# Head of the norm-fed stages widened to four outputs, norm and gate rows moved to PSUM, attention's maximum and scaling regrouped

## The chip, the cores and the metric

The kernel runs on one core of one Trainium2 chip. The metric is device time in microseconds (us) of one execution; lower is better. Input and output are float32, and matmuls take either float32 operands or pairs of float16 parts.

## The reference, cut to what matters

Two transformer blocks run one after the other on a sequence of 512 tokens of width 1024.

```
x   : (1, 512, 1024)
h   = rms_norm(x, g_norm1) * (1 + scale1) + shift1
q, k, v, index rows, pool rows, gates = split(h @ w_in)
y   = sparse attention: 8 heads of 64, 128 keys picked for each query, one k/v head
x   = x + gate1 * ((g_attn * (y @ w_up_attn) + g_pool * (pool @ w_up_pool)) @ w_out)
h2  = rms_norm(x, g_norm2) * (1 + scale2) + shift2
x   = x + gate2 * peer_ffn(h2)          # 16384 experts, 16 of them per head, 8 heads
# second block, two layers
layer 0: windowed attention, 16 heads, 4 k/v heads, distance term slope_h * |i - j|,
         a sink logit per head inside the softmax, window 128 to either side
layer 1: latent attention, 16 heads of 64 + 32 rotary columns, all 512 keys
each layer: h = h + (o * silu(z)) @ w_out
            h = h + (p @ ple_w) * sigmoid(rms_norm(h, ple_norm) @ ple_w_gate)
out = rms_norm(h, final_norm)
```

## The kernel before, in words

Features lie on the 128 partitions: `xT` and `hT` hold 8 blocks of 128 features by 512 tokens. SyncE loads weight tiles of 128x1024 float32 into a ring of 4; POOL cuts each (`cut_tile`, lines 588 to 591) into a high and a low float16 part in a second ring of 4, `parts`; TensorE (PE) multiplies three of the four products of parts (`three`, the matmuls of line 639) and adds them up in PSUM. The order of the tiles is fixed by a plan of stages (`make_plan`), written once and walked by all engines in the same order.

A stage of kind "features" has for each output block `m` its own tile, and runs `m` by `m`, each over 8 input blocks `k`: 24 matmuls of 128x512 for one output. Its sums go to PSUM banks 0 to 3 in turn (`bank`). POOL cuts the tile of output `n` only when PE has begun output `n - 3` (semaphore `begun`), since that is when the slot of output `n - 4` is free. A stage of kind "tokens" runs the other way: for each `k` it adds to four token blocks at once.

A norm works like this. ACT squares the rows of `xT` (line 1014), PE sums them over the partitions with a matrix of ones (`norm_part`, line 689) into bank 7, in `features` stages behind the outputs (`behind`, one part after each output from the third on). ACT takes the root (line 1023), DVE the reciprocal (line 1253). Then for each `k` DVE makes the normed row (`normed`, line 1256) in `whole`, a pair of SBUF rows, ACT writes its high part to `hT` (line 1008 or 1037), and DVE writes the low part (`low`, line 1264 or 1266) and signals `h_ready`. The next stage waits for `h_ready` of block `k` while it runs its first output. The root row and `whole` lie in SBUF (`spare`). The first norm also has, for each `k`, one block of the modulation product on DVE (`modulate`, line 1347, a custom multiply-and-add over 1024 columns with an accumulator).

An attention (`attention` on each engine) walks units of one head and one block of 128 queries, with `w` keys: 128 to 512 in the sparse one (32 units), 256 or 384 in the window one (64 units), 512 in the latent one (64 units). PE's order is fixed: scores of unit `u` (line 738), transposes of the probabilities of `u - 1` (line 747), values of `u - 2` (line 758). DVE adds the mask (1305) or the distance term (1310) in one instruction and takes the negated maximum in a second (1313); in the window one a third, tiny one takes the minimum with the negated sink (1316). ACT takes the exponentials with their sum (1056), in the window one after one of the sink (1053), and copies the transposed probabilities out of PSUM (1008). DVE then adds the sink's term (1325), takes the reciprocal of the sum (1326) and scales the unit's 128x64 output (1328).

After the two later attentions `gate_turned` multiplies each transposed output block by its gate (1668) into `whole` and cuts it into parts (1286, 1287); the stages `a_out` and `b_out` read these. The stages `ple_g0` and `ple_g1` read a norm and give the sigmoid gates (ACT, 1192), which DVE multiplies by the embedding (1684) and adds to `xT` (1686).

## Time and profile before

| what | value |
|---|---|
| median of 3 runs | 2720.87 us (2720.87 to 2723.99) |
| the profiled execution, its own time | 2717.65 us |
| its span, first to last instruction | 2715.8 us |
| mean granted clock of TensorE | 0.968 of full speed |
| share of the chain that ended last | PE 76%, DVE 14%, POOL 3%, issue 3%, ACT 2%, DMA 2% |
| PE busy | 2513.6 us, 93% |
| DVE busy | 1573.1 us, 58% |
| ACT busy | 597.0 us, 22% |
| POOL busy | 1602.8 us, 59% |

Stages in the span, in us from its start: the first norm and the stage `q` 22 to 69, sparse attention 249 to 309, `out` to 420, `peer_q` 429 to 479, the experts to 1893, `a_q` 1902 to 1951, window attention 2016 to 2145, `a_out` 2156 to 2205, `ple_w0` and `ple_g0` 2206 to 2273, the latent projections 2284 to 2409, latent attention 2412 to 2571, `b_out` 2580 to 2630, `ple_w1` and `ple_g1` to 2698, the final norm and the output to the end. Busy time counts only instructions that occupy an engine; an engine can be busy and still wait for another within a stage, so each stage is read by what its slowest chain consists of.

### The profile page before, as it was taken

The numbers are of one execution on the slowest core, as the hardware profiler recorded it, in microseconds if no ns is written. First come the engines' busy times: TensorE is split into PE (matmuls) and PEld (weight loads), VectorE is DVE, ScalarE is ACT, GpSimd is POOL, SyncE is SP. The second block draws the span as 40 slices with busy tenths as digits, with TensorE's granted clock in tenths as the row PEclk, the third lists the DMA queues.
The fourth block names the chain that finished last, engine by engine and source line by source line (L and its number), as shares of the span: only waits on it lengthen the run. The fifth ranks groups of instructions, "written<-read, shape, count | busy, mean of one in ns | idle before, by whom it ended". The sixth has DMA issues, their size and how long they took to land.

```text
span 2715.8 us, 38740 instructions
## 1 busy us (share of the span) xinstructions
PE 2513.6 (93%) x12856; PEld 1259.4 (46%) x12856; DVE 1573.1 (58%) x2831; ACT 597.0 (22%) x1250; POOL 1602.8 (59%) x1048
## 2 busy tenths in 40 slices
PE   4998958999999999999999999999998898999997
PEld 1544523444455555544444444444455533557743
DVE  7896736999877777418822222241228745565534
ACT  2112201211122222211111111111125322245422
POOL 5774137899966666789966666660650166830063
PEclk8998978999999999999999999999999999999998
DMA  6222054355548578688755555550220022310021
GB/s 242 86 86 101 1 209 171 113 153 159 152 128 252 165 222 254 191 277 274 259 203 201 201 201 203 204 203 1 95 78 1 17 73 74 102 54 1 9 78 39
DMA packets 189253, 375.46 MB, mean 138 GB/s; under 512 B 13536, under 2 KB 79200, under 8 KB 189152
## 3 DMA queue, kind: packets, MB, share of 16 engines
q1 hardware_dynamic: 119696, 332.64, 36.3%
q10 hardware_dynamic: 69456, 41.49, 5.2%
q8 instruction: 61, 1.00, 0.2%
q14 instruction: 40, 0.33, 0.0%
HBM read 302.77 MB, written 71.30 MB: 138 GB/s over the span
## 4 chain that ended last, share of the span: by engine, by line
PE 76%; DVE 14%; POOL 3%; issue 3%; ACT 2%; DMA 2%; SPq 0%; DVEq 0%; POOLq 0%; ACTq 0%
PE ps L639 63%; PE ps L738 3%; PE ps L758 3%; PE ps L747 2%; PE ps L870 2%; DVE arena L1347 1%; PE ps L689 1%; DVE spare L1256 1%; POOL ring L589 1%; DVE arena L1465 1%; DVE arena L1464 1%; DVE arena L1286 1%; DVE arena L1313 1%; ACT arena L1056 1%; DVE spare L1253 1%
## 5 line engine op out<-in xcount | busy, mean ns | idle before, releaser
L639 PE MATMUL ps<-hT,parts 128*128 128x512 f16 x4800 | 1068.6, 382 | 38.8 <-DVE hT L1264 22.4
L588 POOL TENSOR_SCALAR parts<-ring 128x1024 f16<-128x1024 f32 x261 | 298.1, 1142 | 873.5 <-PE ps L639 791.6
L639 PEld LDWEIGHTS ps<-hT,parts 128*128 128x128 f16 x4800 | 465.7, 98 | 613.6 <-issue 31.8
L639 PE MATMUL ps<-arena 128*128 128x512 f16 x3072 | 668.2, 381 | 6.9 <-DVE arena L1634 6.9
L591 POOL TENSOR_TENSOR parts<-ring,parts 128x1024 f16<-128x1024 f32 x261 | 573.9, 2199 | 21.8
L639 PEld LDWEIGHTS ps<-arena 128*128 128x128 f16 x3072 | 301.5, 98 | 374.5 <-issue 16.1
L1629 DVE TENSOR_TENSOR arena<-arena 128x512 f32<-128x512 f32 x128 | 144.1, 1126 | 433.4 <-DMA arena<-gate_mem 430.5
L589 POOL TENSOR_SCALAR ring<-ring 128x1024 f32<-128x1024 f32 x261 | 310.5, 1190 | 0.0
L609 POOL TENSOR_TENSOR arena<-ring,arena 128x1024 f16<-128x1024 f32 x128 | 283.1, 2212 | 10.7
L639 PE MATMUL ps<-arena,parts 128*128 128x512 f16 x876 | 207.3, 396 | 46.7 <-POOL parts L591 32.5
L607 POOL TENSOR_SCALAR arena<-ring 128x1024 f16<-128x1024 f32 x128 | 148.0, 1157 | 171.0 <-PE ps L639 171.0
L1120 ACT ACTIVATE spare<-ps 128x512 f32<-128x512 f32 x128 | 76.4, 597 | 575.1 <-PE ps L639 307.6
L1159 ACT ACTIVATE arena<-arena 128x512 f16<-128x512 f32 x128 | 80.5, 630 | 520.8 <-DVE arena L1629 520.7
L1008 ACT ACTIVATE arena<-ps 128x512 f32<-128x512 f32 (+6 forms) x250 | 125.7, 517 | 184.5 <-PE ps L639 182.6
L639 PEld LDWEIGHTS ps<-arena,parts 128*128 128x128 f16 x876 | 87.3, 101 | 169.6 <-issue 59.4
L1605 DVE TENSOR_TENSOR xT<-xT,ps 128x1024 f16<-128x1024 f16 x64 | 78.2, 1221 | 84.8 <-PE ps L870 84.8
L1634 DVE TENSOR_TENSOR arena<-arena 128x512 f16<-128x512 f32 x128 | 122.0, 954 | 5.8 <-ACT arena L1159 5.8
L747 PE MATMUL ps<-ident,arena 128*128 128x128 f32 x496 | 88.2, 289 | 24.2 <-ACT arena L1056 24.0
L747 PEld LDWEIGHTS ps<-ident,arena 128*128 128x128 f32 x496 | 56.8, 142 | 108.4 <-ACT arena L1056 87.2
L639 PE MATMUL ps<-parts,hT 128*128 128x512 f16 (+3 forms) x480 | 73.7, 316 | 33.0 <-DVE hT L1266 23.3
L1310 DVE SCALAR_TENSOR_TENSOR arena<-arena,ps 128x256 f32<-128x256 f32 (+1 forms) x64 | 31.1, 487 | 112.2 <-PE ps L738 110.3
L1014 ACT ACTIVATE hT<-xT 128x512 f32<-128x512 f32 x40 | 24.5, 626 | 297.3 <-DVE xT L1504 217.9
(175 smaller groups left out, 2491.9 us busy)
## 6 DMA issues: line engine op xcount, KB each, us to landing
ring<-w SPq DMA_DIRECT2D x133, 512.0 KB, 3.2
ring<-u SPq DMA_DIRECT2D x128, 512.0 KB, 3.9
ring<-v SPq DMA_DIRECT2D x128, 512.0 KB, 3.3
act_mem<-spare SPq DMA_DIRECT2D x128, 256.0 KB, 3.9
gate_mem<-arena ACTq DMA_DIRECT2D x4, 8192.0 KB, 42.7
arena<-act_mem SPq DMA_DIRECT2D x128, 256.0 KB, 3.6
arena<-gate_mem SPq DMA_DIRECT2D x128, 256.0 KB, 3.8
arena<-ada_w SPq DMA_DIRECT2D x48, 512.0 KB, 6.0
```

The lines of the kernel that those rows point to most:

```text
L588: G.tensor_scalar(dst[:, 0, :], src, WS, 1.0, ALU.mult, ALU.mult).then_inc(scaled, 1)
L589: G.tensor_scalar(src, src, WS, 1.0, ALU.mult, ALU.mult).then_inc(scaled, 1)
L591: G.tensor_tensor(dst[:, 1, :], src, dst[:, 0, :], ALU.subtract).then_inc(parts_ready, 1)
L607: G.tensor_scalar(dst[:, 0, :], src, 1.0, 1.0, ALU.mult, ALU.mult).then_inc(v_high, 1)
L609: G.tensor_tensor(dst[:, 1, :], src, dst[:, 0, :], ALU.subtract).then_inc(parts_ready, 1)
L639: ins = [T.matmul(out_, a, b, start=start and j == 0, stop=stop and j == 2) for j, (a, b) in enumerate(((lhs[0], rhs[0]), (lhs[0], rhs[1]) ...
L738: T.matmul(ps[:, 4 + u % 2, 0:rhs.shape[-1]], lhsT, rhs, start=True, stop=True).then_inc(logits, 1)
L747: mm = T.transpose(ps[:, 6 + u % 2, c * P:(c + 1) * P], probs_b[:, u % 2, c * P:(c + 1) * P], ident[:, :])
L758: mm = T.matmul(ps[:, u % 2, 0:64], pt[:, u % 2, c * P:(c + 1) * P], value_rows(un, un["c0"] + c), start=(c == 0), stop=(c == un["nc"] - 1))
L1008: return A.activation(dst, src, ACT.Copy, scale=scale)
L1629: V.tensor_tensor(prod[:, at % 2, :], pair[:, at % 4, 0, :], pair[:, at % 4, 1, :], ALU.mult).then_inc(product, 1)
L1634: V.tensor_tensor(w_parts[:, at, 1, :], prod[:, at % 2, :], w_parts[:, at, 0, :], ALU.subtract).then_inc(weighted, 1)
```

## The change

Three parts. First, a function `features_wide` runs the first four outputs of a stage together: for `k` 0 to 4 it adds to outputs 0 to 3 at once, then it finishes output 0, 1, 2, 3 over `k` 5 to 7, and the last four run as before. `peer_q`, `a_q`, `a_out`, `ple_g0`, `b_out` and `ple_g1` use it. The parts of the norm's sum come in pairs after outputs 5, 6 and 7. Second, the reciprocal root, the normed rows, the gate rows and the gated row lie in PSUM banks 7, 5 and 6, and 4; `gate_turned` multiplies in place in PSUM. Third, in the sparse and the window attention one `tensor_tensor_reduce` adds the mask or distance and takes the minimum of the negated sum (window: starting from the negated sink, with queries scaled by a per-head factor `steep` at `a_q`'s copy); the sinks' exponentials and, in all three attentions, the reciprocals and the output scaling are done once for eight units, whose values lie side by side in one PSUM bank.

```diff
+        whole_root = ps[:, 7, :]
+        def normed_row(k):
+            return ps[:, 5 + k % 2, :]
+        def gate_row(m):
+            return ps[:, 5 + m % 2, :]
+        gated_row = ps[:, 4, :]
...
+            def features_wide(name, rhs, need, after=None):
+                st = stages[name]
+                early, side = 5, 4
+                def unit(m, k):
+                    return three(bank(st.s0 + m), piece(st.t0 + m, k * P, P), rhs(k), k == 0, k == KC - 1)
+                for k in range(early):
+                    need(k)
+                    for m in range(side):
+                        if k == 0:
+                            need_bank(st.s0 + m)
+                            need_tile(st.t0 + m)
+                        first, last = unit(m, k)
+                        if k == m == 0:
+                            first.then_inc(begun, 1)
+                for m in range(st.outs):
+                    if m >= side:
+                        need_bank(st.s0 + m)
+                        need_tile(st.t0 + m)
+                    for k in range(early if m < side else 0, KC):
+                        if m == 0:
+                            need(k)
+                        first, last = unit(m, k)
+                        if m > 0 and k == (early if m < side else 0):
+                            first.then_inc(begun, 1)
+                    last.then_inc(summed, 1)
+                    if after is not None:
+                        after(m)
...
+            def late_pairs(n):
+                def after(m):
+                    for k in range(2 * (m - 5), 2 * (m - 5) + 2):
+                        if m >= 5:
+                            norm_part(n, k)
+                return after
...
-                    if u0 + u >= 2:
-                        pe.wait_ge(o_ready, u0 + u - 1)
+                    if u % EIGHT == 0 and u0 + u >= 2 * EIGHT:
+                        pe.wait_ge(o_ready, (u0 + u) // EIGHT - 1)
+                    at = place(un) * 64
                     for c in range(un["nc"]):
-                        mm = T.matmul(ps[:, u % 2, 0:64], pt[:, u % 2, c * P:(c + 1) * P],
+                        mm = T.matmul(ps[:, u // EIGHT % 2, at:at + 64], pt[:, u % 2, c * P:(c + 1) * P],
...
-            features("peer_q", hr, h_need(1))
+            features_wide("peer_q", hr, h_need(1))
...
-            features("a_q", hr, h_need(2))
+            features_wide("a_q", hr, h_need(2))
...
-            features("a_out", in_parts(az), lambda k: pe.wait_ge(turned_read, t_a + k + 1), behind(3, 2))
+            features_wide("a_out", in_parts(az), lambda k: pe.wait_ge(turned_read, t_a + k + 1), late_pairs(3))
...
-            features("ple_g0", hr, h_need(3), behind(4, 2))
+            features_wide("ple_g0", hr, h_need(3), late_pairs(4))
...
-                    if un["kind"] == "window":
-                        own.do(A.activation(sm[:, 8 + u % 4:9 + u % 4],
-                                            rows2[:, ROWS2["sink"][0] + un["h"]:ROWS2["sink"][0] + un["h"] + 1],
-                                            ACT.Exp, bias=sm[:, u % 4:u % 4 + 1]))
+                    own.do(A.activation(probs_b[:, u % 2, 0:w], src, ACT.Exp, bias=peak(un, u),
+                                        scale=1.0 if un["kind"] == "latent" else -1.0, accum_out=total(un, u)), probs)
+                    if un["kind"] == "window" and u % EIGHT == EIGHT - 1:
+                        act.wait_ge(sink_shifted, u // EIGHT + 1)
+                        own.do(A.activation(eight_sinks(u), eight_sinks(u), ACT.Exp), sink_exps)
...
-            take("a_q", lambda s, b: copy(aq[:, s, :], b, scale=0.125 / WS))
+            act.wait_ge(rows2_loaded, 16)
+            steep = ROWS2["steep"][0]
+            take("a_q", lambda s, b: copy(aq[:, s, :], b, scale=rows2[:, steep + s:steep + s + 1]))
...
-                own.link(V.reciprocal(root, root))
+                own.link(V.reciprocal(whole_root, root))
                 def normed(k, dst, signal):
-                    own.do(V.scalar_tensor_tensor(out=dst, in0=xT[:, k, :], scalar=g_of(k), in1=root,
+                    own.do(V.scalar_tensor_tensor(out=dst, in0=xT[:, k, :], scalar=g_of(k), in1=whole_root,
...
-                    src = whole[:, k % 2, :]
+                    src = normed_row(k)
...
                     if un["kind"] == "sparse":
-                        own.link(V.tensor_tensor(soft_b[:, u % 2, 0:w], src, mask[:, un["i"], 0:w], ALU.add))
-                        src = soft_b[:, u % 2, 0:w]
+                        own.do(V.tensor_tensor_reduce(out=soft_b[:, u % 2, 0:w], in0=src, in1=mask[:, un["i"], 0:w],
+                                                      scale=-1.0, scalar=HIGHEST, op0=ALU.add, op1=ALU.min,
+                                                      accum_out=peak(un, u)), max_ready)
                     elif un["kind"] == "window":
...
+                        if u % EIGHT == EIGHT - 1:
+                            own.settle()
+                            a_ = ROWS2["sink"][0] + un["h"] - (EIGHT - 1)
+                            own.do(V.tensor_tensor(eight_sinks(u), eight_peaks(u), rows2[:, a_:a_ + EIGHT], ALU.add),
+                                   sink_shifted)
+                    else:
+                        own.do(V.tensor_reduce(peak(un, u), src, AX, ALU.max, negate=True), max_ready)
...
                 def normalise(u):
+                    if u % EIGHT != EIGHT - 1:
+                        return
...
-                    own.do(V.tensor_scalar(out_rows(un), ps[:, u % 2, 0:64], tot, None, ALU.mult), o_ready)
+                    by = tot.unsqueeze(2).broadcast_to([P, EIGHT, 64])
+                    if blocks is None:
+                        own.do(V.tensor_tensor(out_.rearrange("p (e d) -> p e d", d=64),
+                                               src.rearrange("p (e d) -> p e d", d=64), by, ALU.mult), o_ready)
...
-                    own.link(V.tensor_tensor(whole[:, b % 2, :], src, z[:, b, :], ALU.mult))
-                    cut_block(halves(z[:, b, :]), whole[:, b % 2, :], signal=turned_read)
+                    own.link(V.tensor_tensor(src, src, z[:, b, :], ALU.mult))
+                    cut_block(halves(z[:, b, :]), src, signal=turned_read)
...
-                    own.do(V.tensor_tensor(prod_t[:, m % 2, :], gate_t[:, m % 2, :], ple[:, m, :], ALU.mult), sig_used)
+                    own.do(V.tensor_tensor(gated_row, gate_row(m), ple[:, m, :], ALU.mult), sig_used)
```

## Rows read from the trace of the kernel before

**Rows 1.** Windows: stretch, us, busy of PE, PEld, DVE, ACT, POOL; clock; DMA.

```profile
26.00:64.00 38.00, 20.23 (x74) 7.62 (x75) 37.38 (x32) 5.77 (x8) 29.11 (x16) 0.78 0.49 185
...
248.50:309.00 60.50, 54.29 (x307) 38.37 (x305) 42.59 (x128) 31.36 (x96) 0.04 (x1) 0.94 0.18 70
2016.00:2146.00 130.00, 111.50 (x611) 75.00 (x612) 104.98 (x386) 75.79 (x258) 0.00 (x0) 0.96 0.02 5
2412.00:2585.00 173.00, 167.29 (x1060) 123.74 (x1061) 95.90 (x242) 81.05 (x192) 3.87 (x3) 0.98 0.02 4
```

**Rows 2.** Groups of DVE by form, 24 to 64 us, the first norm.

```profile
L1347 DVE CUSTOM_DVE_ANT_0 arena<-arena,route,vecs 128x1024 f32<-128x1024 f32 x8 | 16.3, 2042 | 0.2
L1256 DVE SCALAR_TENSOR_TENSOR spare<-xT,gain,spare 128x512 f32<-128x512 f32 x8 | 13.1, 1643 | 0.3
L1266 DVE SCALAR_TENSOR_TENSOR hT<-spare,ada,hT 128x512 f16<-128x512 f32 x8 | 9.1, 1132 | 0.1
```

**Rows 3.** Groups of DVE by form, 309 to 415 us, operands in PSUM.

```profile
L1347 DVE CUSTOM_DVE_ANT_0 arena<-arena,ps,vecs 128x1024 f32<-128x1024 f32 x22 | 27.0, 1274 | 0.0
...
L1286 DVE TENSOR_SCALAR arena<-ps 128x512 f16<-128x512 f32 x12 | 8.3, 688 | 1.0 <-PE ps L730 0.7
```

**Rows 4.** Groups of PE by form, sparse attention: busy and mean | idle before.

```profile
L747 PE MATMUL ps<-ident,arena 128*128 128x128 f32 x80 | 16.1, 299 | 5.3 <-ACT arena L1056 5.2
```

**Rows 5.** Groups by form, window attention, 2016 to 2146 us.

```profile
L747 PE MATMUL ps<-ident,arena 128*128 128x128 f32 x160 | 32.7, 304 | 17.8 <-ACT arena L1056 17.7
L1053 ACT ACTIVATE arena<-arena 128x1 f32<-128x1 f32 x64 | 18.8, 294 | 50.1 <-DVE arena L1316 50.1
L1313 DVE TENSOR_REDUCE arena<-arena 128x1 f32<-128x384 f32 x32 | 17.7, 553 | 1.1
```

**Rows 6.** Timeline, first unit of the window attention: start, duration, instruction, count, idle before.

```profile
2020.32 0.69 PE L747 MATMUL ps<-ident,arena 128*128 128x128 f32 x2 [2.98 <-ACT arena L1056]
```

**Rows 7.** Timeline, `a_q`.

```profile
1902.24 2.76 PE L639 MATMUL ps<-hT,parts 128*128 128x512 f16 x6 [6.43 <-DVE hT L1264]
...
1903.03 1.36 POOL L588 TENSOR_SCALAR parts<-ring 128x1024 f16<-128x1024 f32 x1 [75.86 <-PE ps L639]
...
1913.72 48.23 PE L639 MATMUL ps<-hT,parts 128*128 128x512 f16 x222 [0.28 <-DVE hT L1264]
...
1915.74 1.04 POOL L588 TENSOR_SCALAR parts<-ring 128x1024 f16<-128x1024 f32 x1 [7.40 <-PE ps L639]
...
1917.88 2.12 POOL L591 TENSOR_TENSOR parts<-ring,parts 128x1024 f16<-128x1024 f32 x1
...
1951.62 0.60 ACT L1008 ACTIVATE arena<-ps 128x512 f32<-128x512 f32 x1 [4.58 <-PE ps L639]
```

**Rows 8.** Timeline, head and end of `ple_g0`.

```profile
2216.02 3.03 DVE L1256 SCALAR_TENSOR_TENSOR spare<-xT,vecs,spare 128x512 f32<-128x512 f32 x2
...
2219.93 0.81 PE L639 MATMUL ps<-hT,parts 128*128 128x512 f16 x3 [1.58 <-DVE hT L1264]
...
2243.21 1.02 PE L689 MATMUL ps<-arena,ones 128*128 128x512 f32 x2
...
2273.60 0.60 ACT L1192 ACTIVATE arena<-ps 128x512 f32<-128x512 f32 x1 [4.92 <-PE ps L639]
```

**Rows 9.** Timeline, first tokens stage behind the fourth norm.

```profile
2284.36 22.87 PE L639 MATMUL ps<-parts,hT 128*128 128x512 f16 x96 [6.43 <-DVE hT L1264]
```

**Rows 10.** Timeline, turned rows and `a_out`.

```profile
2153.49 0.43 DVE L1286 TENSOR_SCALAR arena<-spare 128x512 f16<-128x512 f32 x1
...
2155.61 5.58 PE L639 MATMUL ps<-arena,parts 128*128 128x512 f16 x18
...
2205.45 0.69 DVE L1504 SCALAR_TENSOR_TENSOR xT<-ps,xT 128x512 f32<-128x512 f32 x1 [5.35 <-PE ps L639]
```

**Rows 11.** Timeline, `peer_q`: first matmuls, and DVE's read of output 3.

```profile
428.89 2.82 PE L639 MATMUL ps<-hT,parts 128*128 128x512 f16 x6 [6.68 <-DVE hT L1266]
...
458.26 0.69 DVE L1286 TENSOR_SCALAR arena<-ps 128x512 f16<-128x512 f32 x1 [2.54 <-PE ps L639]
```

More of the change, by code:

```diff
@@ L63 @@
 FAR = 1e32
+HIGHEST = 3e38
 VECS = {}
@@ L434, in build @@
         U_SPARSE, U_WINDOW, U_LATENT = 0, NT * HEADS, NT * (HEADS + A_H)
+        EIGHT = 8
+        O_SPARSE, O_WINDOW, O_LATENT = U_SPARSE // EIGHT, U_WINDOW // EIGHT, U_LATENT // EIGHT
+        O_END = O_LATENT + NT * B_H // EIGHT
         def logit_operands(un):
@@ L453, in value_rows, with place, eight_out @@
             return vlat[:, c, h * VD:(h + 1) * VD]
-        def out_rows(un):
+        def place(un):
             i, h = un["i"], un["h"]
-            t = {"sparse": o_tok, "window": a_tok, "latent": btok}[un["kind"]]
-            return t[:, i, h * 64:(h + 1) * 64]
+            return 2 * i + h % 2 if un["kind"] == "latent" else h % EIGHT
+        def eight_out(un):
+            i, h = un["i"], un["h"]
+            if un["kind"] == "latent":
+                return btok[:, :, (h // 2) * 128:(h // 2) * 128 + 128], NT
+            t = {"sparse": o_tok, "window": a_tok}[un["kind"]]
+            return t[:, i, (h // EIGHT) * 512:(h // EIGHT) * 512 + 512], None
         def soft_buffers(kind):
@@ L463, in soft_buffers, with peak, eight_peaks, total_at @@
             return soft_w, probs_w, probsT_w, small_w
+        def peak(un, u):
+            n = (u // EIGHT % 2) * EIGHT + place(un) + (32 if un["kind"] == "sparse" else 0)
+            return soft_buffers(un["kind"])[3][:, n:n + 1]
+        def eight_peaks(u):
+            n = (u // EIGHT % 2) * EIGHT
+            return small_w[:, n:n + EIGHT]
+        def total_at(un, u):
+            return (u // EIGHT % 2) * EIGHT + {"sparse": 48, "window": 16, "latent": 64}[un["kind"]]
+        def total(un, u):
+            n = total_at(un, u) + place(un)
+            return soft_buffers(un["kind"])[3][:, n:n + 1]
+        def eight_totals(un, u):
+            n = total_at(un, u)
+            return soft_buffers(un["kind"])[3][:, n:n + EIGHT]
+        def eight_sinks(u):
+            n = 32 + (u // EIGHT % 2) * EIGHT
+            return small_w[:, n:n + EIGHT]
         block = ctx.enter_context(nc.Block())
@@ L988, in _ @@
                 turn([(i, btok[:, i, b * P:(b + 1) * P]) for i in range(NT)])
-            features("b_out", in_parts(bz), lambda k: pe.wait_ge(turned_read, t_o + k + 1), behind(5, 2))
+            features_wide("b_out", in_parts(bz), lambda k: pe.wait_ge(turned_read, t_o + k + 1), late_pairs(5))
             features("ple_w1", in_parts(pT), lambda k: pe.wait_ge(p_ready, 2 + k + 1),
                      lambda m: norm_part(5, KC - 3 + m) if m in (1, 2) else None)
-            features("ple_g1", hr, h_need(5), behind(6, 2))
+            features_wide("ple_g1", hr, h_need(5), late_pairs(6))
             last_parts(6, 2)
@@ L1191, in gate @@
                         act.wait_ge(sig_used, (0 if name == "ple_g0" else KC) + s - 1)
-                    return A.activation(gate_t[:, s % 2, :], b, ACT.Sigmoid, scale=1.0 / WS)
+                    return A.activation(gate_row(s), b, ACT.Sigmoid, scale=1.0 / WS)
                 def of_sum(k):
@@ L1261, in low @@
                     dve.wait_ge(h_high, KC * n + k + 1)
-                    src = whole[:, k % 2, :]
+                    src = normed_row(k)
                     if shift_of is None:
@@ L1278, in norm @@
                     if k < KC:
-                        normed(k, whole[:, k % 2, :], norm_whole)
+                        normed(k, normed_row(k), norm_whole)
                     if k >= 1:
@@ L1309, in maxima @@
                         slope = 2.0 ** (-8.0 * (un["h"] + 1) / A_H)
-                        own.link(V.scalar_tensor_tensor(out=soft_b[:, u % 2, 0:w], in0=rows2[:, at:at + w],
-                                                        scalar=-slope, in1=src, op0=ALU.mult, op1=ALU.add))
-                        src = soft_b[:, u % 2, 0:w]
-                    ins = V.tensor_reduce(nm, src, AX, ALU.max, negate=True)
-                    if un["kind"] == "window":
-                        own.link(ins)
-                        ins = V.tensor_tensor(nm, nm, small_w[:, 48 + un["h"]:49 + un["h"]], ALU.min)
@@ L1317, in maxima @@
-                    own.do(ins, max_ready)
+                        own.do(V.tensor_tensor_reduce(out=soft_b[:, u % 2, 0:w], in0=src, in1=rows2[:, at:at + w],
+                                                      scale=-slope, scalar=small_w[:, 48 + un["h"]:49 + un["h"]],
+                                                      op0=ALU.add, op1=ALU.min, accum_out=peak(un, u)), max_ready)
+                        if u % EIGHT == EIGHT - 1:
[5 more added lines that the diff above has]
+                        own.do(V.tensor_reduce(peak(un, u), src, AX, ALU.max, negate=True), max_ready)
@@ L1821, in lay_out @@
     gap = np.abs(np.arange(3 * P)[None, :] - P - np.arange(P)[:, None]).astype(np.float32)
-    dist = np.where(gap <= WINDOW, gap, np.float32(FAR))
+    dist = np.where(gap <= WINDOW, -gap, np.float32(-FAR))
+    steep = np.empty((P, 8), np.float32)
+    for s_ in range(8):
+        for half_ in range(2):
+            h_ = (2 * (s_ // A_G) + half_) * A_G + s_ % A_G
+            steep[half_ * 64:half_ * 64 + 64, s_] = 0.125 / WS * 2.0 ** (8.0 * (h_ + 1) / A_H)
     half = ROPE // 2
```

34 lines of the change are left out of this document (19 added, 15 removed).

## The prediction
> **What bounds the kernel now.** I read the chain that ended last first: PE holds 76% of it and DVE 14% (the table above). The reader is to see that only stretches in which PE waits can give time back, and that DVE is what it mostly waits for. So the windows by stage come next [rows 1]. In the latent attention PE is busy 167.3 of 173 us: nothing to win. In the window attention 111.5 of 130, in the sparse one 54.3 of 60.5, in the first norm 20.2 of 38 while DVE is busy 37.4: there the time is DVE's. The groups by form then tell what ends PE's waits, and the timelines of single stages show how a stage begins.
>
> **The first norm.** Per block `k` DVE issues one modulation product, one normed row and one low part. They take 2.04, 1.64 and 1.13 us on average [rows 2]. With one operand in PSUM the same kinds take 1.27 and 0.69 us while POOL cuts tiles beside them [rows 3]; a row form with a scalar of its own I put at 0.75. The excess over 0.75 is 8 x 0.89 = 7.1 us for the normed rows and 8 x 0.38 = 3.1 us for the low parts: 10.2 us. It comes from two operands in SBUF beside POOL's instructions, busy 29.1 of the 38 us [rows 1]. The change puts root and normed rows in PSUM, so both lose it. The product keeps both operands in SBUF, with an excess of 8 x 0.77 = 6.1 us. I take a gain of 8: most of the 10.2, less something that the product may pick up. What follows (PE on `q`, then DVE's own statistics and picks) starts from here and moves with it. Ends: 0 and 11. The Trainium skill, "SBUF — State Buffer", section "Who interferes with whom", says that VectorE with at most one SBUF input outside its two-port modes does not contend with GpSimd, that with two it does, and that whichever started first holds the shared ports for its whole instruction. The trace agrees: 1.27 against 2.04 us for the product [rows 2, 3]. Taken to its end the rule speaks against part of this gain, since POOL's instructions then meet the product more often; that is the first rival.
>
> **Sparse attention.** PE waits 5.2 us, all for the exponentials, which wait for DVE's maximum [rows 4]. PE's order makes the chain: scores of `u`, DVE, ACT, transposes of `u`, values of `u - 1`, scores of `u + 2`; one DVE pass per two units. The change takes one of two DVE instructions out of it and leaves one with an accumulator read. No row shows that instruction at this width. Nearest is the product, also a custom one: 1.27 us at 1024 columns [rows 3], so about 0.75 at 512 if its time goes by columns, as I take it, because the other forms do; 1.27 if it doesn't; no less than the 0.69 of a plain one. The chain gets some 0.6 us shorter at each pass, the waits are 5.2 / 16 = 0.33 us. So PE becomes the bound and I take the 5.2 less a us at the start, where the window attention pays 3 with a table load [rows 6]: 4.2. At the end one 128x512 scaling stands where a 128x64 one stood: 0.4 us more. Net 3.8; ends 2 and 5.
>
> **Window attention.** PE waits 17.7 us for the exponentials [rows 5]. Of it 3.0 are the first unit's latency and the loading of the function table [rows 6]; they stay. The rest, 14.7 us, is 0.46 us at each of 32 passes. Out of each pass go one instruction of 0.55 us, the tiny minimum, and the sink's exponential ahead of the large one (0.29 us, some of it beside other work; I count 0.2) [rows 5]: over 0.75 us at 384 columns, over 0.6 at 256. That exceeds the wait, so PE bounds here too. The sinks come back once in eight units, on ACT (busy 75.8 of 130) behind the exponential that matters; the scaling of eight units (0.7 us) stands on DVE beside the next scores on PE. Both cost nothing while DVE has this slack: it was busy 105 of 130 and loses instructions; without it each group would cost up to 0.7 us, 5.6 in all. Less 0.4 at the end: gain 14.3. Ends 9 and 15.5. **Latent attention**: PE is the bound, DVE's eight reciprocals and scalings in one change nothing; minus 0.4 for the end.
>
> **The wide stages.** A matmul of 128x512 at full clock takes 48.23 / 222 = 0.217 us [rows 7]; 192 of them are 41.7 us. `a_q` takes 49.4 from its first matmul to the reading of its last output (1902.24 to 1951.62) [rows 7], so 7.7 us are waiting for DVE's rows, or slow clock. With four outputs at once PE has 12 matmuls for each row, 2.6 us at full clock, more than the 1.4 that DVE's two forms of 0.69 take per row [rows 3]. But **tile 3 is not there**. POOL cuts the tile of output 3 only when output 0 has begun: it starts 0.8 us after the first matmul [rows 7], and before nobody needed it for 15 us. Now PE needs it after nine matmuls. A cut without DVE beside it takes 4.26 us (1915.74 to the end of 1917.88 + 2.12) [rows 7], so tile 3 is ready 5.1 us after the first matmul. The nine take 4.1 at the lower clock (0.46 each by the first six) [rows 7]. PE stands for a us, then has 183 x 0.217 = 39.7. Sum 44.8 plus what the clock costs. The granted clock is at its lower level (1.2 of 2.4 GHz) after the norm's gap. The stage behind the fourth norm shows the price: 96 matmuls back to back in 22.87 us, against 20.8 at full clock, 2.1 us lost in all [rows 9]. Part of that is in the nine already; whether the stall of a us makes it start again no row tells, so 0 to 2.1 more, and I take 1. `a_q`: 45.8 for 49.4, gain 3.6 (2.5 to 4.6). The later tiles: POOL begins tile 4 when output 1 resumes, 27 matmuls or 5.8 us before it is needed, for a cut of 4.3: enough.
>
> `peer_q`: output 3 is read 29.4 us after the first matmul [rows 11]; four more outputs at 5.2 make 50.2. By the same working 45.8. But DVE's products (two SBUF operands) run beside POOL and stretch its cuts to about 5.3, under 5.8 with little left. Gain 4 (1 to 5).
>
> `ple_g0`: the first two normed rows take 3.03 us beside POOL [rows 8] where two take 1.4 without, so the first matmul comes 1.6 us earlier; that was PE's whole wait of 1.58. From there to the last reading: before 53.7 us (2219.93 to 2273.60) [rows 8]. After: PE is at full clock, its nine matmuls take 2 us and it stands 3.1 us for tile 3; 5.1 + 39.7 = 44.8; four pairs of sum-of-squares matmuls ahead of the last output where five stood, 1.02 us each at most [rows 8], 4.1; 1 for the clock, which may fall in the stall: 49.9. Gain 3.8 + 1.6 = 5.4. `ple_g1` is the same: 10.8 for both (6 to 14).
>
> `a_out`, `b_out`: here the rows were ahead of PE, since it first turns all eight. The stage took 49.8 us [rows 10]. In place in PSUM, the cut reads PSUM and takes 0.69 [rows 3] where it took 0.43 [rows 10]; the first matmul waits for four of them, 1 us later. Then 44.8 + 4.1 = 48.9 plus 0 to 2.1 for the clock. With the 1: 49.9 to 52. I take a loss of 0.7 each, 1.4 for both (5 lost to 1 won). The stall for tile 3 eats what the width gives.
>
> **The sum.** 8 + 3.8 + 14.3 - 0.4 + 3.6 + 4 + 10.8 - 1.4 = 42.7 us. The profiled execution took 2717.65, so 2675 for one like it; the median shown is 3.2 us above, 2720.87, and 2678 is my number for the median. The expert stages (479 to 1893) hold nothing that the change touches and move as a block.
>
> **The rivals.**
> 1. *The contention only moves.* DVE's normed rows get out of POOL's way, but the modulation product then starts behind a POOL instruction each time. Where that is POOL's longest, 2.12 us [rows 7], eight of them have 17 us of excess where there are 6.1 now: 10.9 more against 10.2 less, and the first norm gains nothing. Total 34.7, so 2686. For it: POOL is busy 77% of that window [rows 1]. Against it: POOL finishes its tiles earlier when it is not blocked itself, and then has none to cut.
> 2. *The combined instruction costs the same at every width*, 1.27 us [rows 3]. At 384 columns it replaces two of 0.55 and the small ones, some 1.5 us of chain [rows 5]; by columns that is some 1.2 at 256 and, in the sparse one without the small ones, 0.6 at 128. Window gain then 4, sparse a loss of 4: total about 25, so 2696. Against it: every other DVE form here goes by its columns.
> 3. *It is slower.* One mechanism: the combined instruction takes two passes over its data and 2.4 us. Its place is the chain of both attentions, once in two units: 48 times about 1 us more, 48 us lost where 18 were won; with the other terms (25 won) that ends 23 us slower, 2744. It decides from about 1.9 us. Against it: the product at 1024 columns takes 1.27 with its accumulator.
> 4. *The width doesn't do what it says*, because tile 3 comes late and the clock drops in each of the six heads: five us of clock more, 2683, inside the range.
>
> **How the numbers follow.** My forecast with rival 4 folded in 0.67; rival 1 0.22; rival 2 0.08; rival 3 0.03. The range: the lower ends of the terms (0 + 2 + 9 + 2.5 + 1 + 6 - 5 - 0.4 = 15) give 2706, the upper ones 2666; all at once are unlikely, and unknown gains of a few us where PE's share of the chain shrinks may be missing. I say 2660 to 2702. A measurement of this kernel tells 0.2%, 5.4 us, from no change. All cases but rival 3 are faster by more than that; between them little is left for no change: 0.96, 0.01, 0.03.
>
> **What would show it.** Right: in the window attention PE's waits ahead of the transposes near 3 us; the combined instruction near 0.6 at 384 columns; normed rows near 0.7 everywhere; each wide stage with nine matmuls, a gap closed by POOL's tile 3 of 1 us (3 in the gate stages), then none; `a_out` no shorter. Wrong: a combined instruction above 1 us; PE waiting in the wide stages for POOL after output 3; a modulation product near 3 us on average; the stretch from 70 to 249 us longer than before.

## The result and the profile after

The changed kernel takes 2654.31 us (median of 4 runs, 2650.83 to 2654.95) where the one before takes 2721.90 beside it: 0.9748 of the time, 95% interval 0.9731 to 0.9765. Forecast were 2678 us and a range of 2660 to 2702. The direction was right, the size was not: 67.6 us were gained, 42.7 had been summed up. The profiled executions have spans of 2715.8 and 2652.1 us, so 63.7 us are in the traces.

First the page of the changed kernel: busy time of the engines, and the chain that ended last.

```profile
PE 2480.6 (94%) x12856; PEld 1263.1 (48%) x12856; DVE 1429.8 (54%) x2439; ACT 585.2 (22%) x1194; POOL 1589.2 (60%) x1048
...
PE 79%; DVE 10%; POOL 5%; issue 3%; DMA 2%; ACT 1%; SPq 0%; POOLq 0%; DVEq 0%; ACTq 0%
```

DVE's share of the chain fell from 14% to 10%, as it should; POOL's rose from 3% to 5%, which the heads of the wide stages below explain. But PE is busy for 2480.6 us where it was for 2513.6, and it issues the same matmuls. That is the trail to the missing gain. The windows by stage show where it lies; columns as in [rows 1]. The kernel before, with the bounds on the same events (first norm, sparse, window and latent attention):

```profile
12.00:69.84 57.84, 33.69 (x112) 12.94 (x112) 52.92 (x53) 13.50 (x22) 37.03 (x21) 0.85 0.57 224
...
249.94:309.55 59.61, 53.83 (x304) 38.30 (x304) 42.18 (x128) 31.36 (x96) 0.00 (x0) 0.94 0.18 71
...
2016.21:2145.43 129.22, 110.93 (x608) 74.43 (x609) 104.45 (x385) 75.63 (x257) 0.00 (x0) 0.96 0.02 5
...
2412.05:2571.24 159.19, 157.66 (x1016) 118.19 (x1016) 83.35 (x222) 81.05 (x192) 0.00 (x0) 1.00 0.01 1
```

The same four stretches of the changed kernel:

```profile
12.00:56.50 44.50, 33.06 (x112) 13.17 (x112) 39.62 (x53) 13.21 (x22) 33.93 (x20) 0.88 0.71 281
...
238.62:291.40 52.78, 50.33 (x305) 39.08 (x305) 19.03 (x72) 31.35 (x96) 0.00 (x0) 0.94 0.21 80
...
1993.24:2097.04 103.80, 99.59 (x608) 75.24 (x609) 44.42 (x161) 64.64 (x201) 0.00 (x0) 0.97 0.02 6
...
2357.61:2512.95 155.34, 153.41 (x1016) 118.97 (x1016) 68.60 (x110) 81.04 (x192) 0.00 (x0) 1.00 0.00 1
```

Take the length of a stretch apart into PE's busy and idle time. Window attention: 25.4 us shorter, of which 14.1 are idle time (18.3 to 4.2) and 11.3 are **busy** time, for the same 608 matmuls at nearly the same clock. Sparse: 6.8 shorter, 3.3 idle and 3.5 busy. Latent: 3.8 shorter, the idle time even 0.4 longer, 4.2 busy. The idle parts are what the prediction said, to half a us: 14.3, 3.8 and -0.4. The busy parts, 19 us in all, are what it lacked.

How a wait gets into the busy time shows in PE's timeline. The kernel before, one unit of 384 columns (the scores L738, the transposes L747, the values L758, and the next scores):

```profile
2071.80 0.86 PE L738 MATMUL ps<-arena 128*128 128x384 f32 x2
2072.85 0.55 PE L747 MATMUL ps<-ident,arena 128*128 128x128 f32 x3 [0.18 <-ACT arena L1056]
2073.23 0.87 PE L758 MATMUL ps<-arena 128*128 128x64 f32 x6
2073.94 0.86 PE L738 MATMUL ps<-arena 128*128 128x384 f32 x2
```

The same unit of the changed kernel:

```profile
2043.11 0.86 PE L822 MATMUL ps<-arena 128*128 128x384 f32 x2
2043.81 0.49 PE L831 MATMUL ps<-ident,arena 128*128 128x128 f32 x3
2044.14 0.81 PE L843 MATMUL ps<-arena 128*128 128x64 f32 x6
2044.79 0.86 PE L822 MATMUL ps<-arena 128*128 128x384 f32 x2
```

The two score matmuls are shown with 0.86 us in both. But after them the transposes start 0.70 us behind the scores' start where nothing is waited for, and 1.05 us behind where something is: 0.35 us later, and the profile calls 0.18 of it idle. The shown end of a matmul lies some 0.16 us behind the moment from which the next could have started. So each wait hides about 0.16 us. PE lists 58 such waits in the window attention before and 3 with the change: 55 fewer make 9 us of the 11.3. From start to start this unit took 2.14 us and takes 1.68 (its neighbours took 2.14 to 2.17 and take 1.64 to 1.84). Of the 0.46 us, 0.35 lie ahead of the transposes; the other 0.11 are the two steps behind them (0.38 to 0.33 and 0.71 to 0.65 us), and why these got shorter no run tells.

The first norm, DVE's groups by form, the counterpart of [rows 2] (the product stands twice: its eight instructions beside the rows, and all sixteen of the stage, whose mean was 1662 before):

```profile
L1446 DVE CUSTOM_DVE_ANT_0 arena<-arena,route,vecs 128x1024 f32<-128x1024 f32 x8 | 13.4, 1674 | 0.2
L1446 DVE CUSTOM_DVE_ANT_0 arena<-arena,route,vecs 128x1024 f32<-128x1024 f32 x16 | 23.2, 1477 | 9.6 <-DMA arena<-ada_w 9.4
L1342 DVE SCALAR_TENSOR_TENSOR ps<-xT,gain,ps 128x512 f32<-128x512 f32 x8 | 6.0, 755 | 0.3
L1352 DVE SCALAR_TENSOR_TENSOR hT<-ps,ada,hT 128x512 f16<-128x512 f32 x8 | 6.0, 746 | 0.1
```

Normed rows and low parts fell to 0.755 and 0.746 us (the prediction took 0.75): 10.2 us. The product got cheaper too, by 3.0 in all (1674 ns for 2042 beside the rows). The stage is 13.3 shorter. The one behind it gives 2.0 back (33.5 us, now 35.5): POOL is busier there (32.4 us, before 28.0) and cuts tiles beside DVE's last group of that stage, eight scalings of key rows with two SBUF operands, which take 5.54 us together where they took 3.06. The prediction had named a longer stretch from 70 to 249 us as a sign against it; this is that sign, and it costs 2.0.

The combined instruction in the window attention, and the scaling of eight units:

```profile
L1396 DVE CUSTOM_DVE_ANT_0 arena<-ps,arena 128x384 f32<-128x384 f32 x32 | 19.8, 618 | 29.6 <-PE ps L822 29.6
L1396 DVE CUSTOM_DVE_ANT_0 arena<-ps,arena 128x256 f32<-128x256 f32 x32 | 15.4, 483 | 124.6 <-PE ps L822 124.6
L1422 DVE TENSOR_TENSOR arena<-ps,arena 128x512 f32<-128x512 f32 x8 | 5.5, 692 | 1.9 <-PE ps L843 1.5
L1396 DVE DVE_READ_ACCUMULATOR2_ANT arena<- 128x1 f32 x64 | 5.3, 83 | 0.0
```

It goes by its columns: 0.618 us at 384, 0.483 at 256. The sparse attention's form costs less still:

```profile
L1390 DVE CUSTOM_DVE_ANT_0 arena<-ps,arena 128x512 f32<-128x512 f32 x8 | 5.5, 692 | 10.1 <-PE ps L822 10.0
```

That is what the plain addition of the mask took at 512 columns (0.691 us), and at 384 it takes 0.556, the same as the plain one. The prediction had put it at 0.75 for 512.

The heads of two wide stages, `a_q` and `ple_g0`, in PE's timeline:

```profile
1883.75 3.52 PE L685 MATMUL ps<-hT,parts 128*128 128x512 f16 x9 [6.32 <-DVE hT L1350]
1888.95 16.35 PE L685 MATMUL ps<-hT,parts 128*128 128x512 f16 x75 [1.69 <-POOL parts L637]
...
2170.27 2.12 PE L685 MATMUL ps<-hT,parts 128*128 128x512 f16 x9
2175.26 10.09 PE L685 MATMUL ps<-hT,parts 128*128 128x512 f16 x46 [2.88 <-POOL parts L637]
```

Nine matmuls, a wait for POOL's tile 3, and then none: as predicted, 1.69 us for the one foreseen and 2.88 for the three. `peer_q` is different. It waits 1.39 us for tile 3 and then twice more:

```profile
442.26 5.34 PE L685 MATMUL ps<-hT,parts 128*128 128x512 f16 x24 [0.71 <-POOL parts L637]
448.31 10.54 PE L685 MATMUL ps<-hT,parts 128*128 128x512 f16 x48 [0.70 <-POOL parts L637]
```

The cuts that it waits for take 6.1 us beside DVE's products, more than the 5.8 that were there for them. With 1.34 us in `a_out`, 2.18 in `b_out` and 2.87 in `ple_g1`, PE's listed waits for POOL's tiles in the six stages are 13.8 us. The clock did not fall in the wait of `ple_g0`: the 46 matmuls behind it take 0.22 us each.

### The profile page after: what moved, and what is told of

Its sections match the earlier page's. It is cut to its first block, busy times and chain, and to the rows that moved or that the text cites. A ratio compares the mean times of both kernels' runs of the same rounds, so it can differ in the third digit from the quotient of the medians.

```text
span 2652.1 us, 37828 instructions
## 1 busy us (share of the span) xinstructions
PE 2480.6 (94%) x12856; PEld 1263.1 (48%) x12856; DVE 1429.8 (54%) x2439; ACT 585.2 (22%) x1194; POOL 1589.2 (60%) x1048
## 4 chain that ended last, share of the span: by engine, by line
PE 79%; DVE 10%; POOL 5%; issue 3%; DMA 2%; ACT 1%; SPq 0%; POOLq 0%; DVEq 0%; ACTq 0%
PE ps L685 64%; PE ps L822 4%; PE ps L843 4%; PE ps L831 2%; PE ps L955 2%; POOL ring L635 1%; POOL parts L637 1%; PE ps L766 1%; DVE arena L1446 1%; DVE arena L1564 1%; DVE arena L1563 1%; DVE arena L1372 1%; DVE arena L1373 1%; POOL parts L634 1%; DMA ring<-w 1%
## 5 line engine op out<-in xcount | busy, mean ns | idle before, releaser
L685 PE MATMUL ps<-hT,parts 128*128 128x512 f16 x4800 | 1054.7, 380 | 29.7 <-POOL parts L637 10.2
L635 POOL TENSOR_SCALAR ring<-ring 128x1024 f32<-128x1024 f32 x261 | 296.9, 1138 | 0.0
L1396 DVE CUSTOM_DVE_ANT_0 arena<-ps,arena 128x256 f32<-128x256 f32 (+1 forms) x64 | 35.1, 550 | 154.2 <-PE ps L822 154.2
```

Of the source, the lines that this page charges most:

```text
L635: G.tensor_scalar(src, src, WS, 1.0, ALU.mult, ALU.mult).then_inc(scaled, 1)
L685: ins = [T.matmul(out_, a, b, start=start and j == 0, stop=stop and j == 2) for j, (a, b) in enumerate(((lhs[0], rhs[0]), (lhs[0], rhs[1]) ...
```

## The experiments

All durations of stages below are windows between the same events of ScalarE's instructions in each trace; a dip of the granted clock moves one by up to 1.7 us, so the clock is named where it matters. "Theory A" differs from run to run and is stated in each.

**1. Two steps for the maximum again**, the rest of the change kept (the sign of the distances, the scale of the exponential and the scaling of the queries are set to match).

```diff
-  V.tensor_tensor_reduce(out=soft, in0=src, in1=mask, scale=-1.0, scalar=HIGHEST, op0=ADD, op1=MIN, accum_out=peak)
+  V.tensor_tensor(soft, src, mask, ADD); V.tensor_reduce(peak, soft, MAX, negate=True)
-  V.tensor_tensor_reduce(..., in1=dist, scale=-slope, scalar=sink, op0=ADD, op1=MIN, accum_out=peak)
+  V.scalar_tensor_tensor(soft, dist, slope, src, MULT, ADD); V.tensor_reduce(peak, soft, MAX, negate=True)
+  V.tensor_tensor(peak, peak, sink, MIN)
```

> The changed kernel with mask or distance and maximum in two instructions again (and the sink's minimum in a third), the scaling and the sinks still once for eight units. Theory A: PE's waits were longer than their idle column says, because the shown end of a matmul lies about 0.16 us behind the moment the next could start; the chain per pass is what counts. Then a pass of two window units goes from 3.44 to about 4.1 us at 384 columns and from 2.70 to about 3.2 at 256: the window attention grows from 103.8 to about 120 us, the sparse one by about 5, the whole to 2677 (2670 to 2682), while PE's listed waits in the window rise by only some 8 us. Rival B: what won more than forecast was the grouping in eights; then this kernel stays within 5 us of the changed one, 2654 to 2660.

Measured: 2680.3 us, ratio 0.9841 (0.9823 to 0.9860). Theory A has the time right, but not its split. Its window attention (the profiled execution took 2687.06):

```profile
2002.53:2125.86 123.33, 104.03 (x608) 73.19 (x608) 81.09 (x225) 64.64 (x201) 0.00 (x0) 0.99 0.02 5
```

19.5 us longer than with the change, though the clock is higher; and again not all is idle time (19.3 against 4.2), 4.4 are busy time. Theory A expected about 8 us of listed waits, and 15.1 came. The reason is their number: PE waits 33 times here, at every second unit and for longer, where it waited 58 times before. That also tests the hidden piece: 30 more waits than with the change, at 0.16 us each, make 4.8 us, and 4.4 were found. Sparse attention is 8.4 longer (61.17, with the clock at 0.89, so that a dip of the clock is in it). So the combined instruction carries most of both.

**2. The kernel before, with the preparation of the next head ahead of the scaling** in DVE's order, and nothing else.

```diff
-  if u >= 2: normalise(u - 2)
-  if hook is not None: hook(u)
+  if hook is not None: hook(u)
+  if u >= 2: normalise(u - 2)
```

> The kernel before, with one swap on DVE in the latent attention: the copies of the next head's rows come ahead of the reciprocal and scaling of the unit two back, which wait for PE's values. Nothing else. Theory A: one unit of each head had PE wait 0.28 us that no idle column shows, since the head's copies stood behind that scaling and pushed the next maximum; the latent attention falls from 159.2 to about 155.3 us, the whole by 4, to 2717. Rival B: the grouping won there by taking 56 reciprocals and scalings off DVE; then the swap does nothing (0 to 1 us).

Measured: 2717.84 us, ratio 0.9983 (0.9973 to 0.9992). Its latent attention:

```profile
2418.31:2573.42 155.11, 153.59 (x1016) 119.01 (x1016) 83.32 (x222) 81.05 (x192) 0.00 (x0) 1.00 0.01 1
```

155.1 for 159.2: the whole gain that the change made there (155.3), from an order that the eight-unit scaling changes as a by-product. How it came about stands in the trace of before, engines PE and DVE in the latent attention:

```profile
2438.03 1.08 PE L738 MATMUL ps<-arena,spare 96*128 96x512 f32 x2
...
2438.33 0.28 DVE L1328 TENSOR_SCALAR arena<-ps,arena 128x64 f32<-128x64 f32 x1 [0.62 <-PE ps L758]
...
2438.53 0.68 DVE L1735 COPY spare<-ps 96x512 f32<-96x512 f32 x1
...
2439.13 0.68 DVE L1735 COPY arena<-ps 96x512 f32<-96x512 f32 x1
...
2439.72 0.68 DVE L1313 TENSOR_REDUCE arena<-ps 128x1 f32<-128x512 f32 x1
2440.22 1.08 PE L738 MATMUL ps<-arena,spare 96*128 96x512 f32 x2
...
2441.27 0.66 PE L747 MATMUL ps<-ident,arena 128*128 128x128 f32 x4
...
2442.70 1.08 PE L738 MATMUL ps<-arena,spare 96*128 96x512 f32 x2
```

The copies of the next head stand behind a scaling that waits for PE, and the next maximum stands behind the copies. That unit takes 2.48 us from scores to scores (2440.22 to 2442.70) where its neighbour takes 2.19, and no row shows any idle time: the transposes start 1.05 us behind the scores and not 0.91, which the shown end covers.

**3. Root and normed rows of the first norm back in SBUF**, rows in PSUM in the later norms.

```diff
-  src = normed_row(k)
+  src = whole[:, k % 2, :] if n == 0 else normed_row(k)
-  own.link(V.reciprocal(whole_root, root))
+  own.link(V.reciprocal(root if n == 0 else whole_root, root))
```

> The changed kernel with root and normed rows of the first norm alone in SBUF again. Theory A: the first norm gives 13.3 us up to the stage after q, of which 2 are lost again where POOL catches up with its cuts beside DVE's statistics; so this kernel is 11 us slower than the changed one, 2665 (2663 to 2668), and the modulation product is back at 2.0 us on average from 1.67. Rival B: the early gain is not kept, because later work has its own clock; then 2654 to 2658.

Measured: 2662.35 us, ratio 0.9782 (0.9761 to 0.9803); 8.0 us lost, between the two theories and nearer to A. Its first norm, DVE by form:

```profile
L1450 DVE CUSTOM_DVE_ANT_0 arena<-arena,route,vecs 128x1024 f32<-128x1024 f32 x16 | 26.1, 1662 | 10.0 <-DMA arena<-ada_w 9.8
L1346 DVE SCALAR_TENSOR_TENSOR spare<-xT,gain,spare 128x512 f32<-128x512 f32 x8 | 13.1, 1643 | 0.3
L1356 DVE SCALAR_TENSOR_TENSOR hT<-spare,ada,hT 128x512 f16<-128x512 f32 x8 | 9.1, 1132 | 0.1
```

Every mean of before is back, the product's too (1662 for 1477). So the rows in PSUM relieve the product as well; nothing moved to it. Of 13.6 us lost at the end of this norm, 2.0 come back in the next stage, where DVE's eight scalings take 3.06 us again, and 4.5 more over the rest of the trace, in steps of some 1.7 us at most; the largest lie where the two traces have different clocks (sparse attention: 1.00 here, 0.94 with the change; `b_out`: 0.94 and 0.92).

**4. One output at a time at the head of all six wide stages**, rows and gates kept in PSUM; the parts of the norm's sum stand one behind each output again.

```diff
-  features_wide("a_q", hr, h_need(2))
+  features("a_q", hr, h_need(2))
...
-  features_wide("ple_g0", hr, h_need(3), late_pairs(4))
+  features("ple_g0", hr, h_need(3), behind(4, 2))
```

> The changed kernel with the six wide stages run output by output again, norm parts one behind each output. Theory A: with rows in PSUM DVE gives one in 1.39 us without interruption, so a stage run output by output waits only 7 x 1.39 less 7 x 0.65 at its head; the width wins little beyond that since PE stands for tile 3: about 2 in a_q, 1 in peer_q, 3 in each gate stage, 0 in a_out and b_out, together 9: 2663 (2659 to 2667). Rival B: the width itself holds most of the 22 us that these stages became shorter: 2672 or more.

Measured: 2654.72 us, ratio 0.9752 (0.9734 to 0.9770): the same as the change within the spread of the runs. Both theories missed; four outputs at once are worth nothing that can be measured here. The head of `ple_g0` says why:

```profile
2168.37 0.81 PE L685 MATMUL ps<-hT,parts 128*128 128x512 f16 x3
2169.66 0.82 PE L685 MATMUL ps<-hT,parts 128*128 128x512 f16 x3 [0.49 <-DVE hT L1350]
2171.05 0.82 PE L685 MATMUL ps<-hT,parts 128*128 128x512 f16 x3 [0.56 <-DVE hT L1350]
...
2176.58 11.94 PE L685 MATMUL ps<-hT,parts 128*128 128x512 f16 x54 [0.56 <-DVE hT L1350]
```

With one output PE waits for each of six rows, 0.49 to 0.56 us by its idle time, and starts one every 1.38 us where three matmuls at full clock take 0.65: 18 matmuls stand in the 8.2 us to 2176.58, and 4.3 of these are lost. With four outputs it stands 2.88 us once, for tile 3. And the two stages that had their rows ready, `a_out` and `b_out`, are no better for four outputs (61.1 and 61.6 us, here 61.5 and 60.3). What the four won in `a_q` and the gate stages, 1.3 + 1.5 + 1.5 us, they lost again in `b_out` and, in these two traces, in the expert stages (1422.5 us, here 1419.6), where the cause is open. So most of the gain of the wide stages as built came from rows and gates in PSUM, 18.5 of the 22.6 us in `peer_q`, `a_q` and the two gate stages: `ple_w0` with `ple_g0` took 78.3 us before, 72.4 in this run and 70.9 with the change.

**5. Three outputs at once** in place of four, and so no tile that isn't cut.

```diff
-  early, side = 5, 4
+  early, side = 5, 3
```

> The changed kernel with three outputs at the head instead of four; nothing else. Theory A: PE's stall for tile 3 (1.4 to 1.7 us in four of the stages, 2.9 in the two gate stages) is the price of the fourth output, which buys nothing: nine matmuls for a row take 1.95 us at full clock, DVE gives a row in 1.39. Without it the gate stages win 2.9 each, a_q, a_out, b_out some 1 each (the lower clock goes on where PE stood), peer_q 1 to 2.5, since POOL may also cut tile 4 earlier: 2643 (2640 to 2648). Rival B: PE then waits for DVE's rows or starts the clock's rise later and nothing is won: 2652 to 2656.

Measured: 2635.97 us, ratio 0.9681 (0.9665 to 0.9697), 18.3 us faster than the change. Theory A has the direction, and its 2643 is 7 us too slow. PE's timeline at the start of `a_q` and of `ple_g0`:

```profile
1880.06 20.26 PE L685 MATMUL ps<-hT,parts 128*128 128x512 f16 x85 [6.32 <-DVE hT L1350]
...
2162.40 17.87 PE L685 MATMUL ps<-hT,parts 128*128 128x512 f16 x82
```

No wait is left: three tiles are there when the stage begins, and nine matmuls per row, 2.0 us, exceed DVE's 1.38. Each of the six stages is shorter: `a_q` by 1.5, `a_out` by 1.5, `ple_g0` by 3.0, `b_out` by 2.9, the last by 3.0, `peer_q` by 2.6. In `a_q` and `ple_g0` that is the wait for tile 3 that the change has there (1.69 and 2.88 us), in `peer_q` it is its three waits for POOL (2.8 us); in `b_out` it is more than the wait of 2.18, since the clock was higher too (0.94 for 0.92). The six together are 14.5 us shorter, and the waits that are gone were 13.8. The other 3.5 us between the two traces lie in stages that this edit does not touch.

**6. Three outputs, and a faster head of `a_out` and `b_out`**: the first four gated blocks in SBUF, where POOL has nothing to cut, and the embeddings cut behind them.

```diff
+  gated_block = whole[:, b % 2, :] if b < 4 else src
-  own.link(V.tensor_tensor(src, src, z[:, b, :], MULT)); cut_block(halves(z[:, b, :]), src, ...)
+  own.link(V.tensor_tensor(gated_block, src, z[:, b, :], MULT)); cut_block(halves(z[:, b, :]), gated_block, ...)
-  cut_embeddings(1); gate_turned(az, "a_z")
+  gate_turned(az, "a_z"); cut_embeddings(1)
```

> As the kernel with three outputs, and two edits ahead of a_out and b_out: the first four turned blocks are multiplied into the SBUF rows as before the change (their cut takes 0.43 instead of 0.69 us, and POOL is idle then), and the first embedding is cut after the turned rows instead of ahead of them. Theory A: the first matmul of a_out and b_out comes 1 us earlier each by the first edit, a_out's 2.2 us earlier by the second: 2639 (2636 to 2643). Rival B: the embedding's cut then collides with POOL's and delays the first residual, or the rows of the last four blocks come too late: no faster than with three outputs.

Measured: 2633.56 us, ratio 0.9671 (0.9654 to 0.9687), the fastest here: 20.8 us under the change, 2.4 under run 5. These 2.4 are less than the 4 that theory A gave the two edits, and the intervals of the two ratios overlap, so that the times alone do not show them; the stages do. The stretch around `a_out` fell from 59.6 to 56.6 us (at a clock of 0.97 for 0.91, which is a part of it), the one around `b_out` from 58.7 to 57.6. From the start of the turning to the first matmul of `a_out` it is 8.98 us, with the change 11.26. DVE ahead of `a_out`:

```profile
2091.31 0.69 DVE L1768 TENSOR_TENSOR spare<-ps,arena 128x512 f32<-128x512 f32 x1 [0.82 <-PE ps L814]
2092.04 0.43 DVE L1372 TENSOR_SCALAR arena<-spare 128x512 f16<-128x512 f32 x1
2092.50 0.69 DVE L1373 SCALAR_TENSOR_TENSOR arena<-spare,arena 128x512 f16<-128x512 f32 x1
```

The cut takes 0.43 us from SBUF and 0.69 from PSUM, as [rows 10] and [rows 3] had it. In its trace the latent attention is 1.7 longer at a clock of 0.98, which hides a part of the gain in the trace.

**7. The combined instruction alone**, added to the kernel before (with the negated distances and the scaled queries that it needs); sinks and scalings one by one.

```diff
-  V.scalar_tensor_tensor(soft, dist, -slope, src, MULT, ADD); V.tensor_reduce(nm, soft, MAX, negate=True)
-  V.tensor_tensor(nm, nm, sink, MIN)
+  V.tensor_tensor_reduce(out=soft, in0=src, in1=dist, scale=-slope, scalar=sink, op0=ADD, op1=MIN, accum_out=nm)
...
-  V.tensor_tensor(soft, src, mask, ADD); V.tensor_reduce(nm, soft, MAX, negate=True)
+  V.tensor_tensor_reduce(out=soft, in0=src, in1=mask, scale=-1.0, scalar=HIGHEST, op0=ADD, op1=MIN, accum_out=nm)
```

> The kernel before with one part of the change alone: mask or distance, maximum and the sink's bound come from the one combined instruction in the sparse and the window attention. Sinks' exponentials, reciprocals and scalings stay one per unit, order and all stages else as before. Theory A (the parts of the chain add up, since PE was waiting for far more than its idle time says): sparse attention gets the whole 6.8 us that it got with the change; window attention what the run with two steps lost, 19.5 of 25.4 us, since the sink's exponential of 0.29 us still stands in each pass; latent nothing. Sum 26: 2696 us, 2692 to 2699. Rival B (PE is already its own bound once the combined instruction is there, and the grouping in eights brings nothing): window the whole 25.4: 2690 us or less. Rival C, my prediction's working (PE's listed idle time is all there is to win): sparse 3.8, window at most 14.3: 2704 us.

Measured: 2692.72 us, ratio 0.9891 (0.9875 to 0.9908); 27.5 us gained, 26 expected by A. Its sparse and its window attention:

```profile
250.82:303.29 52.47, 50.28 (x304) 38.97 (x304) 27.49 (x129) 31.35 (x96) 0.00 (x0) 0.93 0.21 81
...
2012.46:2120.85 108.39, 103.08 (x609) 74.76 (x609) 68.91 (x321) 75.62 (x257) 0.00 (x0) 0.97 0.02 6
```

Sparse has the whole gain (52.5; 52.8 with the change). The window has 20.8 of 25.4. Grouping by eight added 4.6 on top, and 5.9 without it (run 1): the parts add up, so neither hides the other. The prediction's working (rival C, 2704) is out.

**8. Two outputs at once**, as in run 5 with `side = 2`.

> The changed kernel with two outputs at once in place of four at the head of the six wide stages. Theory A: what the width has to give is time for DVE's rows. With two outputs PE takes six matmuls or 1.3 us per row, DVE 1.44, and for rows 5 to 7 PE then takes only 0.65 us each, so that it waits for row 7 some 2.5 to 3 us in a_q, ple_g0 and ple_g1 and perhaps in peer_q; tile 3 is not waited for. Against three outputs (2636 us) that loses 8 to 12: 2646 us, 2642 to 2650; with four outputs it was 2654. Rival B (only tile 3 matters, the rows are fast enough in PSUM, as the run with one output seemed to say): 2636 us, within 2.

Measured: 2638.53 us, ratio 0.9702 (0.9686 to 0.9718). A's 2646 missed; B's "within 2" is missed by half a us, but it is far nearer. DVE brings a row every 1.38 us, not 1.44, and PE takes six matmuls for it, 1.3 us at full clock and more at the lower one at which `a_q` starts. A wait of 0.56 us is all that `ple_g0` shows. So two or three outputs are enough, and one is too few (run 4); the fourth is what costs.

## Why the prediction was right or wrong

**Window attention: the step that failed.** The prediction took PE's listed waits as all that could be won there: "The rest, 14.7 us, is 0.46 us at each of 32 passes", and "That exceeds the wait, so PE bounds here too". The listed idle time indeed fell by 14.1 us. But PE's busy time fell by 11.3 as well, because each of the 58 listed waits began behind a matmul whose shown end lies about 0.16 us too late: 9 us by the 55 waits that are gone; run 1 bears the piece out, and some 2.5 us stay unexplained. The upper end of 15.5, made from the same column, shut the true value out. The rest of the mechanism was right: the chain got shorter, PE is the bound, and the remaining wait ahead of the transposes is 2.6 us (3 foreseen), 2.3 of which are the first unit's latency.

**Sparse attention** has the same error: 3.8 predicted, 3.3 fell as idle, 6.8 in all. Rival 2, the same 1.27 us at every width, is out: the instruction goes by its columns, from 0.292 us at 128 to 0.692 at 512.

**Latent attention**: "PE is the bound, DVE's eight reciprocals and scalings in one change nothing". It gained 3.8. A delay of 0.29 us per head stood in the trace before, without any idle time; only the starts show it. Run 2 gives the cause, an order of DVE's instructions. Together these three mis-sized terms are 18.4 of the 21 us that the spans lie apart from the sum (63.7 against 42.7). The first norm and the wide stages came 6.3 us better than their terms, and `out`, the experts and the latent projections took 3.7 longer, where the cause is open.

**First norm**: 8 predicted, 13.3 came, 2.0 went back in the next stage. The rows' own part was 10.2, as worked out. The step that failed is the "something that the product may pick up": it lost 3. That also settles rival 1, which had the contention move to the product: its mean beside the rows went from 2042 to 1674 ns, not up to 3000. The rule of the Trainium skill, "SBUF — State Buffer", section "Who interferes with whom", is that VectorE with at most one SBUF input, outside its two-port modes, does not contend with GpSimd, and that with two it does. The rows here agree with it: 0.75 us with one beside POOL, 1.64 with two. Why the product gained (it still has two SBUF operands, and still takes longer than the 1.27 us with one in PSUM [rows 3]), fewer of POOL's instructions meeting it or meeting it at a better moment, was not tried and stays open.

**The wide stages** came near as totals: `a_q` 4.5 (3.6 predicted), `peer_q` 3.2 (4), the two gate stages with the `ple_w` ahead of them 14.9 (10.8), `a_out` and `b_out` -2.6 (-1.4). Tile 3's stall was foreseen with its place and its size. Three terms were wrong beneath the totals. In `peer_q` the later tiles were called enough, with POOL's cut under 5.8 us, and PE waited 0.71 and 0.70 us for two of them; the prediction had named such a wait as a sign against it. The clock was taken to cost 1 us after the stall and cost nothing. And the gain was put to the width, when run 4 shows that the rows in PSUM bring most of it and that four outputs at once bring nothing net: the stall eats about all that the width gives, which run 5 puts at some 18 us.

**Rival 3** (slower, at 2.4 us per combined instruction) fell at 0.618 us. **Rival 4** half came true, the stall without the clock. Of the range, the text itself named "unknown gains of a few us where PE's share of the chain shrinks"; they were 18, and were the first thing to work out, not the last. (Its upper ends add up to 2665 us, where it says 2666.)

## What to carry to other kernels

Where an engine waits often and shortly, price the stretch from start to start of its instructions against the same ones in a place where nothing is waited for; its idle column misses a piece of every wait, here about 0.16 us, which made some 9 of the window attention's 25.4 us. Look at the longest unit of a repeated loop even where no idle time is shown. And give an engine's head of a stage only as many outputs side by side as there are tiles ready: with three of them the stages ran without a wait, with four they lost about all that the width gave.

## What was new of the hardware

- The combined instruction with its accumulator takes 618 ns at 128x384 and 483 at 128x256 from PSUM and SBUF, plus a read of 83 ns: a plain pass of 554 and 420 with 64 more, so it replaces two passes for one. The sparse attention's form takes 556 and 422 ns at these widths, no more than a plain pass. The two differ in their start value, a tile's column in the one and a constant in the other; whether that makes the 64 ns no run shows.
- DVE's product with both operands in SBUF got faster (1662 to 1477 ns) when its neighbours on the same engine had an operand moved to PSUM, and went back to 1662 when that was undone (run 3), though POOL is no less busy beside it (34 of 44.5 us, before 37 of 57.8).
- PE's granted clock was still at its full 2.4 GHz after waits of 2.88 us (46 matmuls in 10.09 us behind one, granted clock 1.00 from 2175.3 to 2185.0), in a stage that began with nine matmuls at full speed.
